# First layer's expert rounds: the second half of a round's down projection placed behind the next round's gate and up projection

## The reference

```
def moe_ffn(h, router_w, router_bias, w_gate, w_up, w_down, sh_gate, sh_up, sh_down):
    scores = sigmoid(h @ router_w)                 # 64 experts
    idx = top_k(scores + router_bias, 8)
    gates = scores[idx] / sum(scores[idx]) * 2.5
    # for each expert e and each token that chose it:
    hid = silu(x @ w_gate[e]) * (x @ w_up[e])      # 1024 -> 256
    y = (hid @ w_down[e]) * gate                   # 256 -> 1024
    # routed = sum of y over a token's 8 experts
    shared = (silu(h @ sh_gate) * (h @ sh_up)) @ sh_down
    return routed + shared
```

## Time and profile before

| | |
|---|---|
| median of 3 runs | 1924.78 us (1920.3 to 1927.61) |
| the profiled execution's own time | 1922.82 us |
| its span | 1921.0 us |
| TensorE matmuls busy | 1690.0 us, 88% of the span |
| VectorE busy | 572.4 us, 30% |
| ScalarE busy | 310.1 us, 16% |
| DMA | 560.50 MB, mean 292 GB/s |
| weights of the experts and other direct loads (q1) | 512.20 MB, 66.7% of 16 engines' span |
| indirect gathers and scatters (q0) | 43.62 MB, 6.0% |
| mean granted TensorE clock | 0.952 |

### The profile page before, as it was taken

The page is one execution under the profiler, slowest core; times in us unless marked ns, Lnnn a source line. Parts: engine busy times, 40 slices in busy tenths (PEclk is TensorE's granted clock), DMA queues, the critical chain, the costliest instruction groups (busy, mean ns, idle before and its releaser), DMA issues. The chain is left out here.

```text
span 1921.0 us, 23595 instructions
## 1 busy us (share of the span) xinstructions
PE 1690.0 (88%) x8663; PEld 775.1 (40%) x8663; DVE 572.4 (30%) x1357; ACT 310.1 (16%) x682; POOL 207.5 (11%) x197
## 2 busy tenths in 40 slices
PE   4999998999999999999995499788789989979895
PEld 2544554564334433334432244454433333333331
DVE  2041666345222222222210551474311111111112
ACT  2101443121111111111110111171101001000011
POOL 0300333000111111111110000030000000000000
PEclk7998999989999999999998699898899999999998
DMA  9323784208899999999993933102599999999992
GB/s 354 118 82 130 269 310 175 72 18 325 350 399 409 418 418 407 417 412 401 417 409 148 393 132 137 42 1 77 214 419 394 419 419 400 419 420 419 420 403 87
DMA packets 125188, 560.50 MB, mean 292 GB/s; under 512 B 17266, under 2 KB 22785, under 8 KB 74896
## 3 DMA queue, kind: packets, MB, share of 16 engines
q1 hardware_dynamic: 106960, 512.20, 66.7%
q0 software_dynamic: 17248, 43.62, 6.0%
q10 hardware_dynamic: 864, 3.15, 0.4%
HBM read 549.94 MB, written 26.80 MB: 300 GB/s over the span
## 5 line engine op out<-in xcount | busy, mean ns | idle before, releaser
L1530 PE MATMUL ps<-wb,pool 128*32 128x512 f32 (+2 forms) x2608 | 485.3, 597 | 19.3 <-issue 19.1
L1530 PEld LDWEIGHTS ps<-wb,pool 128*32 128x32 f32 (+2 forms) x2608 | 160.0, 124 | 305.4 <-issue 305.3
L1544 DVE TENSOR_TENSOR ffn_hid<-ffn_sg,ps 128x256 f32<-128x256 f32 x71 | 29.9, 422 | 606.9 <-ACT ffn_sg L1538 606.9
L1574 PE MATMUL ps<-pool,ffn_hidT 128*32 128x512 f32 (+2 forms) x584 | 165.9, 604 | 23.7 <-DVE ffn_hidT L1559 10.8
L1574 PE MATMUL ps<-hT,ffn_hidT 128*32 128x512 f32 (+2 forms) x680 | 157.7, 599 | 19.6 <-DVE ffn_hidT L1559 14.6
L1437 POOL DMA_INDIRECT pool<-h_rows,ffn_index x71 | 74.6, 1051 | 649.4 <-DVE ffn_index L1487 328.4
L2166 PE MATMUL ps<-wb,hT 128*128 128x512 f32 x320 | 139.7, 598 | 1.6 <-issue 1.6
L1538 ACT ACTIVATE ffn_sg<-ps 128x256 f32<-128x256 f32 x71 | 27.2, 383 | 487.9 <-PE ps L1530 487.9
L1574 PE MATMUL ps<-sh_wd,ffn_hidT 128*32 128x512 f32 (+2 forms) x272 | 100.3, 597 | 4.7 <-DVE ffn_hidT L1559 2.6
L1500 PEld LDWEIGHTS ps<-const,pool 128*128 128x128 f32 x568 | 77.5, 194 | 66.1 <-issue 62.7
L1592 PE MATMUL ps<-x_res,rw 128*128 128x512 f32 x224 | 103.1, 603 | 0.9 <-ACT x_res L1620 0.9
(11 more groups left out here) (291 smaller groups left out, 1828.0 us busy)
## 6 DMA issues: line engine op xcount, KB each, us to landing
wb<-in_expert_w_gate_dram SPq DMA_DIRECT2D x108, 1024.0 KB, 12.9
wb<-in_expert_w_up_dram SPq DMA_DIRECT2D x108, 1024.0 KB, 18.4
pool<-in_expert_w_down_dram SPq DMA_DIRECT2D x52, 1024.0 KB, 19.1
hT<-in_expert_w_down_dram SPq DMA_DIRECT2D x52, 1024.0 KB, 17.4
wb<-in_ada_w_dram SPq DMA_DIRECT2D x24, 2048.0 KB, 10.1
sh_wd<-in_expert_w_down_dram SPq DMA_DIRECT2D x24, 1024.0 KB, 19.8
mix_yr<-y_rows SPq DMA_DIRECT2D x8, 2048.0 KB, 11.7
wb<-in_diff_w_in_dram SPq DMA_DIRECT2D x6, 2048.0 KB, 16.7
```

Source lines behind the costliest of these rows:

```text
L1530: mm = nc.tensor.matmul(core.ps[lo:lo + width, gu_bank(n), :], xT[:, n % 2, k, lo:lo + width], w[:, k], start=k == 0, stop=k == KD - 1, sk ...
L1574: mm = nc.tensor.matmul(core.ps[lo:lo + width, down_bank(half), :], hidT[:, n % 2, k, lo:lo + width], wd_at(q % DR, half, k), start=k == 0 ...
```

## The change

It touches only the first layer's order (`not last`); the second layer's lists come out as before.

- TensorE: gate and up of n, then **the second down half of n-1**, [info], hidden values of n, both halves of the tokens of n+1, first down half of n. After the loop the second down half of the last round.
- VectorE: the copy of the turned hidden values of n comes ahead of the copy of the next tokens' first half.
- ScalarE: silu of n comes ahead of the second output half of n-1.

SyncE's and GpSimd's lists are as before.

```diff
@@ scalar
                 for n in range(R):
+                    act_silu(act, n)
                     if n >= 1 and not last:
                         act_y(act, n - 1)
-                    act_silu(act, n)
@@ vector
                     dve_hidden(dve, n)
-                    if n + 1 < R:
+                    if last and n + 1 < R:
                         dve_take_x(dve, n + 1)
                     dve_take_hidden(dve, n)
+                    if not last and n + 1 < R:
+                        dve_take_x(dve, n + 1)
@@ tensor
                 for n in range(R):
                     pe_gate_up(pe, n)
-                    if last and n >= 1:
-                        pe_sum(pe, n - 1)
-                    if n % BATCH == 0 and n // BATCH + 1 < plan.batches:
-                        pe_info(pe, n // BATCH + 1)
-                    if n + 1 < R:
-                        pe_turn(pe, n + 1, 0)
-                    pe_turn_hidden(pe, n)
                     if last:
+                        if n >= 1:
+                            pe_sum(pe, n - 1)
+                        if n % BATCH == 0 and n // BATCH + 1 < plan.batches:
+                            pe_info(pe, n // BATCH + 1)
+                        if n + 1 < R:
+                            pe_turn(pe, n + 1, 0)
+                        pe_turn_hidden(pe, n)
                         pe_down(pe, n, 0)
-                    if n + 1 < R:
-                        pe_turn(pe, n + 1, 1)
-                    for half in range(1 if last else 0, 2):
-                        pe_down(pe, n, half)
+                        if n + 1 < R:
+                            pe_turn(pe, n + 1, 1)
+                        pe_down(pe, n, 1)
+                    else:
+                        if n >= 1:
+                            pe_down(pe, n - 1, 1)
+                        if n % BATCH == 0 and n // BATCH + 1 < plan.batches:
+                            pe_info(pe, n // BATCH + 1)
+                        pe_turn_hidden(pe, n)
+                        if n + 1 < R:
+                            pe_turn(pe, n + 1, 0)
+                            pe_turn(pe, n + 1, 1)
+                        pe_down(pe, n, 0)
                 if last:
                     pe_sum(pe, R - 1)
+                else:
+                    pe_down(pe, R - 1, 1)
```

## The result

| | median | runs |
|---|---|---|
| before | 1922.60 us | 1917.77 to 1928.13, 20 runs |
| after | 1928.19 us | 1925.27 to 1935.32, 20 runs |

The ratio is 1.0029, with a 95% interval of 1.0019 to 1.0040: the change made the kernel 5.6 us slower. That is less than the 0.5% named in the prediction, but outside of what the runs leave open, and on the other side of the 3 us gain that was forecast. The profiled execution has a span of 1925.9 us (before: 1921.0). Of all runs behind this document two, one of the kernel before (2322.9 us) and one of lag_fill (3009.8 us), showed a much lower granted clock and are left out.

The account below looks back on a forecast made before the run. The prediction took the full DMA engines to bound the first-layer loop: -4.3 us of filled dips, +0.7 tail and +0.6 held loads make -3.0, so 1921.8 us from a median of 1924.8, range 1909 to 1932.

Parts of the forecast that it names:

- a DMA share far under 0.97 behind a held load: Sign of being wrong: DMA engines' busy share under 0.97 behind a delayed down-weight load would mean the queue ran dry.
- a clock below 1 in the loop: Sign of being wrong: TensorE's granted clock, 1.00 throughout the first-layer loop before, falling below 1 there.
- What bounds the loop: First layer's 43 rounds: the DMA engines are full, share 0.99 to 1.01 at 406 to 413 GB/s, and set the pace.
- TensorE's saving: TensorE in the loop: 25 us of hidden-value waits go, less 5 to 7 for tile-width changes; about 18 us, 0.43 per round.
- The seam: TensorE where tile width changes: next weight load at 0.84 instead of 0.27 us; net 0.17 each, 5.4 us in all.
- The tail: Behind the last gate and up projection: one more down half there makes the end 0.7 us later.
- SyncE's queue: Down-weight loads issued later, holding loads behind them at most 2 us; taken as 0 cost, 1 us in a few places.
- rival (2): Held down loads let the DMA queue run dry, with under about 4.5 us queued; 14 us longer, 1936; chance 0.07.
- Rival (3): Longer waits for weights pull TensorE's clock down, about 12 rounds at 3.4 us; 17 us longer, 1939; chance 0.05.
- The sum: Whole kernel: 4.3 us less DMA idle time, 0.7 more tail, 0.6 for held loads; net -3.0 us.
- The dip at 550: DMA share of 0.89 for 12 us around 550 us, 1.4 us of DMA time, forecast to fill entirely.

Follow-up runs that it names:

- lag_fill: after_lag with two additional 128x512 matmuls (four in the last round) ahead of eight gate and up projections that waited for weights: 1923.19 us, ratio 1.0001.
- the light pair: Kernel before and changed kernel, each loading only half of each first-layer expert's gate and up weights (wrong output, timing only): 1910.86 and 1881.95 us.
- after_lag: Changed kernel with SyncE's first-layer queue reordered, next expert's gate and up loads ahead of this expert's down load: 1925.13 us, ratio 1.0003.
- before_lag: Kernel before with the same reordered SyncE queue, gate and up loads ahead of the down load, TensorE's order old: 1924.95 us, ratio 1.0001.
- before_hold: Kernel before with one more wait on SyncE's queue, holding down loads until the following round's gate and up projection is done: 1925.17 us, ratio 1.0005.
- before_early: Kernel before with the first layer's first gate and up projection moved ahead of the last shared down projection: 1929.02 us, ratio 1.0024.
- after_fill: Changed kernel with three additional 128x512 matmuls ahead of the gate and up projection of ten rounds that waited for weights: 1927.22 us, ratio 1.0023.
- after_tail: Changed kernel with the second down half (and ScalarE's output half) back in its old place ahead of the last round only: 1928.11 us, ratio 1.0027.
- after_pairs: Changed kernel with second down half and ScalarE's output half back in the old place ahead of rounds beginning two experts: 1924.99 us, ratio 1.0011.

## Why the prediction was wrong

The measured time lies inside the stated range, but the change went the other way than forecast. Two of the prediction's own signs of being wrong came: a DMA share far under 0.97 behind a held load, and a clock below 1 in the loop.

**What bounds the loop: right.** With full loads the transfers set the pace; the light pair shows it, and after_lag against before_lag: 1925.1 and 1925.0 us.

**TensorE's saving: right in kind, too small.** 18 us were worked out, 28.9 are measured with the light loads (31.4 in the loop's stretch). The waits go as described, and a round without a wait comes to 12.09 where the sum had 12.85 - 0.43 = 12.42. Part of the missing 0.3 us lies ahead of the down projection: its first weight load stood 0.28 to 0.44 us behind the transposes and stands 0.13 behind them now (511.86 behind 511.73), while the sum took only the 6.9 us by which its matmuls stood. The rest was not taken apart. The seam costs what it was priced at: 0.84 + 1.05 = 1.89 us for a down half with it, 1.88 by the sum. The Trainium skill, TensorEngine Tiling (Array Packing), "Key Properties", says that a change of the tiling mode drains TensorE. The trace agrees, with a gap of 0.84 instead of 0.27 us, of which 0.2 us are left as net cost.

**The tail: right in the profile.** 0.7 us were forecast; 11.57 - 9.24 = 2.33 less 1.62 of clock is 0.7.

**SyncE's queue: this step failed.** It said "So I take 0", from 5.2 us of queued work at the tightest place in the trace of before. That number belongs to a TensorE that is late for its weights. Once TensorE stands and waits for them, there is only as much behind the awaited load as the rings have free slots, and the time to the next issue is the whole gate and up projection, the down half that was moved behind it and the issue itself: from 638.08 to 655.41 in round 13. At the end of that projection (652.94) the queue was about to run dry, where rival (2) asked for less than 4.5 us of work left. So rival (2), which had 0.07, is what happened, with a size below its 14 us: the three windows on dips above come to 0.5, 1.6 and 1.8 us of DMA time against a share of 1.01. The rows of before that stood for the queue's depth were not valid for the state that the change itself makes. Held loads alone cost nothing measurable (before_hold, 1.0005), and with the gate loads let past them the loss goes (after_lag, 1.0003 against 1.0029): it takes both the earlier TensorE and the held loads.

**Rival (3), the clock: it was real and got 0.05.** The prediction said that waits of 24 us would gather in rounds of 2 to 3 us each and took comfort from 1.00 at waits up to 2.4. They were 33.6 us, nine of them of 2.2 to 5.1 us, and behind six of these, of 2.41 to 5.08 us, the clock was at half. So the 2 to 3 us a wait were about right, and the comfort was not: before_early lost the clock behind 2.38 us, where before had kept it behind 2.39. Rival (3)'s price was overrated. It took 3.4 us for each of 12 rounds, 41 us in all; six projections came out 1.6 to 2.9 us longer than 7.1, 11 us in all. They cost where they delay the freeing of slots, and in the last round, 1.6 us.

The Trainium skill, TensorE: Matmul & The Clock Gate, "HAM oscillation", says that short compute between waits for DMA makes the clock fall in every turn of a loop. The trace agrees in that the clock falls at such waits, though here it fell in six rounds of 43, each 54 us or more behind the last. The rule should have had more weight than a row from a kernel whose waits were shorter.

**The sum.** DMA idle time was to fall by 4.3 us. The dip at 550 did fill, but those behind rounds 8, 13, 20, 24 and 35 came: the last weights landed 1.8 us later instead of 4 us earlier. Of that 6 us error and the 1.6 us of clock in the tail the queue's order accounts for the most (after_lag, 5 us by the ratios), the clock for 1 to 3.7 (after_fill). The two overlap: in the profile of after_lag the clock fell less often too and stayed up in the last round. How they share the loss is not settled.

No kernel here with the full loads beats before by more than its runs differ. A sixth slot for down weights, the other way to end the holding, wasn't tried.

## What to carry to other kernels

When transfers and TensorE are both full, work taken off TensorE turns into waits for data, and the question is no longer what TensorE saves but what each moved instruction frees: a slot released one step later holds its own load and every load queued behind it. Read the depth of the queue not from the kernel before but for the state after the change, with the consumer standing and waiting: what the rings still allow in flight, against the time from there to the next release. Order the loads so that one whose slot comes free late stands behind the ones that are needed first.

## What the runs showed of the hardware

- In the changed kernel's loop TensorE's clock was at half (1.2 GHz) behind waits of 2.41, 2.52, 2.70, 2.95, 3.57 and 5.08 us, and stayed at full (2.4 GHz) behind 2.19, 2.27 and 2.59; before kept it behind 2.39, before_early lost it behind 2.38. Over all profiles the two groups overlap widely: after_tail lost it behind 2.33 us, after_lag kept it behind 3.52 and after_pairs behind 3.73. So the length of the wait alone doesn't tell what the clock will do. The gate and up projection with a fall took 8.4 to 10.0 us instead of 7.1. The shortest wait with a fall (after_tail) and the longest without (after_pairs), each with its window:

```profile
907.80 8.63 PE L1531 MATMUL ps<-wb,pool 128*32 128x512 f32 x64 [2.33 <-issue]
905.00:921.00 16.00, 13.67 (x96) 4.81 (x94) 2.36 (x5) 1.66 (x3) 1.91 (x2) 0.89 1.01 419
```

```profile
1028.10 7.09 PE L1531 MATMUL ps<-wb,pool 128*64 128x512 f32 x32 [3.73 <-issue]
1024.00:1040.00 16.00, 10.62 (x50) 4.11 (x50) 1.53 (x3) 1.07 (x2) 0.97 (x1) 1.00 0.15 60
```

- Three 128x512 matmuls in the wait kept the clock up in all ten rounds where they stood (after_fill); in six of the ten it had fallen in the changed kernel.
- Passing from 32-wide to 64-wide tiles moves the next weight load from 0.27 to 0.84 us behind the last (508.66 in the changed kernel), but a group of 4 steps then needs 1.05 instead of 1.43 us for its loads: net about 0.2 us.
- The start of the loop differed by up to 7 us between profiles of kernels with the same code ahead of it, more than the effect measured here.
